# Dilated attention: 66 moving columns instead of 128 in the products of probabilities with v

## The reference, cut to what matters

```python
def _dilated_branch(q, k, v, window, dilation):
    ...
    sc = jnp.where(mask, sc, -jnp.inf)
    m = jnp.max(sc, -1)
    p = jnp.exp(sc - m[..., None])
    l = jnp.sum(p, -1)
    o = jnp.einsum('bhrnqk,bhrnkd->bhrnqd', p, vb.astype(F32)) / l[..., None]
```

## Time and profile before

| what | value |
|---|---|
| runs: median (lowest to highest of 3) | 2781.31 us (2777.66 to 2781.51) |
| profiled execution: span from first to last instruction | 2786.4 us |
| PE busy | 2702.5 us, 97% of the span |
| PEld busy | 2277.9 us, 82% |
| DVE busy | 2107.3 us, 76% |
| ACT busy | 1287.9 us, 46% |
| POOL busy | 343.9 us, 12% |

### The profile page before, as it was taken

The page is one execution under the profiler, slowest core; times in us unless marked ns, Lnnn a source line. Parts: engine busy times, 40 slices in busy tenths (PEclk is TensorE's granted clock), DMA queues, the critical chain, the costliest instruction groups (busy, mean ns, idle before and its releaser), DMA issues. The chain is left out here.

```text
span 2786.4 us, 44753 instructions
## 1 busy us (share of the span) xinstructions
PE 2702.5 (97%) x17355; PEld 2277.9 (82%) x17355; DVE 2107.3 (76%) x3262; ACT 1287.9 (46%) x2296; POOL 343.9 (12%) x273
## 2 busy tenths in 40 slices
PE   9999988989999999999999999899999999999998
PEld 7888877888888888888878887788877888888886
DVE  6644445775799999898889885366658999998978
ACT  5323345853454444443356754566543544444332
POOL 0000056340000000000000001365511000000001
PEclk9999999999999999999999999999999999999999
DMA  5323252534322222284322433532042122224652
GB/s 184 121 106 116 81 178 94 151 99 161 119 79 91 83 91 76 107 327 144 107 102 106 152 93 124 175 124 93 18 167 108 63 84 81 91 78 177 238 189 90
DMA packets 162444, 339.08 MB, mean 122 GB/s; under 512 B 35584, under 2 KB 69568, under 8 KB 151616
## 3 DMA queue, kind: packets, MB, share of 16 engines
q1 hardware_dynamic: 143664, 321.54, 32.6%
q10 hardware_dynamic: 18576, 14.75, 1.7%
HBM read 252.17 MB, written 84.05 MB: 121 GB/s over the span
## 5 line engine op out<-in xcount | busy, mean ns | idle before, releaser
L2494 POOL TENSOR_TENSOR ffn_down_rstd<-ffn_down_rstd,ffn_down_power 128x1 f32<-128x1 f32 x15 | 15.0, 1000 | 1263.2 <-DVE ffn_down_rstd L2430 1263.2
L1051 DVE TENSOR_TENSOR even_in_w_lo<-even_in_raw_left,even_in_w_hi 128x512 fp32r<-128x512 f32 x80 | 49.9, 686 | 88.2 <-ACT even_in_w_hi L976 88.2
L934 PE MATMUL even_in_acc<-even_in_w_hi,even_x_hi 128*128 128x512 f32 x256 | 99.6, 389 | 0.0
L935 PE MATMUL even_in_acc<-even_in_w_lo,even_x_hi 128*128 128x512 f32 x256 | 99.6, 389 | 0.0
L936 PE MATMUL even_in_acc<-even_in_w_hi,even_x_lo 128*128 128x512 f32 x256 | 99.6, 389 | 0.0
L4024 DVE SCALAR_TENSOR_TENSOR even_mixed<-even_mixed,odd_qkv_taps 128x1023 f32<-128x1023 f32 (+2 forms) x72 | 92.1, 1281 | 4.9 <-ACT even_mixed L3857 3.2
L3508 DVE CUSTOM_DVE_ANT_0 dil_probs<-dil_bank,dil_mask 128x128 f32<-128x128 f32 (+1 forms) x192 | 56.0, 347 | 38.9 <-PE dil_bank L3417 32.2
L936 PE MATMUL even_in_acc<-even_in_w_hi,even_in_s_lo 128*128 128x512 f32 x192 | 74.7, 389 | 0.0
L934 PE MATMUL even_in_acc<-even_in_w_hi,even_in_s_hi 128*128 128x512 f32 x192 | 74.7, 389 | 0.0
L935 PE MATMUL even_in_acc<-even_in_w_lo,even_in_s_hi 128*128 128x512 f32 x192 | 74.7, 389 | 0.0
L3464 ACT ACTIVATE dil_probs<-dil_probs,dil_neg_peak 128x128 f32<-128x128 f32 (+1 forms) x192 | 70.7, 442 | 2.6 <-DVE dil_neg_peak L3513 2.6
(11 more groups left out here) (881 smaller groups left out, 9221.1 us busy)
## 6 DMA issues: line engine op xcount, KB each, us to landing
ffn_w_raw<-in_ffn_up SPq DMA_DIRECT2D x42, 1024.0 KB, 4.8
even_mixed<-in_ffn_down SPq DMA_DIRECT2D x28, 512.0 KB, 4.1
odd_mixed<-in_ffn_down SPq DMA_DIRECT2D x28, 512.0 KB, 4.0
hp<-even_in_stage SPq DMA_DIRECT2D x13, 1024.0 KB, 4.2
hidden<-even_mixed SPq DMA_DIRECT2D x22, 512.0 KB, 2.6
ffn_w_raw<-in_od_w_qkv SPq DMA_DIRECT2D x11, 1024.0 KB, 5.7
hidden<-odd_mixed SPq DMA_DIRECT2D x22, 512.0 KB, 2.6
even_in_raw_left<-in_ev_w_in SPq DMA_DIRECT2D x10, 1024.0 KB, 5.0
```

Of the source, the lines that this page charges most:

```text
L934: pe.matmul(to, hi[:, tok], wh, start=(opens and k == 0), stop=False, skip_group_check=not opens)
L935: pe.matmul(to, hi[:, tok], wl, start=False, stop=False, skip_group_check=not opens)
L1051: dve.tensor_tensor(w_lo[:, p % 2, k], source(i)[:, k], f32(w_hi[:, p % 2, k]), ALU.subtract).then_inc(lo_ready, 1)
```

## The change

The window of v that streams past the stationary probabilities becomes 66 columns wide (`DIL_OUT`). An even head's window starts at its own first value (64 values, its ones, and the first value of the next head). An odd head's starts one column ahead of its first value, at the ones of the head before (those ones, 64 values, its own ones). The result goes to the first 66 columns of the head's place in PSUM, and the copy of the odd heads reads from column 1 instead of 63. The two lines with a matmul become a loop over the one or two blocks of keys, in the same order. The stationary operand, the number of matmuls, the semaphores and all other programs are as before.

```diff
         def v_window(u, h):
 
-            at = h // 2 * 2 * (DIL_HD + 1) + 2 * (h % 2)
-            return v[:, v_slot(u)].rearrange("p h e -> p (h e)")[:, at:at + P]
+            at = h // 2 * 2 * (DIL_HD + 1) + DIL_HD * (h % 2)
+            return v[:, v_slot(u)].rearrange("p h e -> p (h e)")[:, at:at + DIL_OUT]
...
-                    if has_before(u):
-                        pe.matmul(o_ps[:, h], probs_t[:, 2 * h], v_window(u - 1, h), start=True, stop=False)
-                    mm = pe.matmul(o_ps[:, h], probs_t[:, 2 * h + 1], v_window(u, h), start=not has_before(u), stop=True)
+                    for b in range(0 if has_before(u) else 1, 2):
+                        mm = pe.matmul(o_ps[:, h, 0:DIL_OUT], probs_t[:, 2 * h + b], v_window(u - 1 + b, h),
+                                       start=b == 0 or not has_before(u), stop=b == 1)
...
-                    at = parity * (DIL_HD - 1)
+                    at = parity
                     dve.tensor_copy(mine[:, :, 0:DIL_HD + 1], heads[:, :, at:at + DIL_HD + 1]).then_inc(o_copied, 1)
```

## The result

The changed kernel took 2789.55 us (median of 20 runs, 2775.21 to 2792.69), the kernel before 2781.69 us beside it (20 runs, 2775.95 to 2787.20). The ratio is 1.0022, with a 95% interval of 1.0014 to 1.0030: slower by 0.2%, where no change was forecast, and the median is 2.6 us above the range. The ratio is the one on record; the quotient of the two medians is 1.0028. A second measurement gave 1.0018 (1.0007 to 1.0030).

A forecast was written before the change was run, and what follows sets the result against it. PE was taken to bound the stage, with stationary loads setting its pace. All terms were taken as 0, leaving 2786.4 us on the profiled execution, 2781 us on the median's scale; range 2775 to 2787 us.

The forecast's parts named there:

- The pace: Products: the 128-column stationary load sets 112 ns a pass before and after, so 560 passes save 0 us.
- the rival of the moving stream: Products: the moving columns set the pace, 52 ns less a pass, 2752 to 2763 us; chance 0.06.
- The formula of the Trainium skill: Products: matmul gap (N / 2.4 + 2.5) ns, 56 for 128 columns and 30 for 66, giving about 2767 us.
- The group ends: Last product of each of 24 units: `o_done` 0.05 to 0.11 us earlier; taken as 0, bound -2.6 us.
- The clock step: Granted clock under the half filled stream: cost unknown, taken as 0; above, one or two more falls, 3.4 us.
- The clock rival: Eleven two-block units' product runs: clock falls in each, 11 x 1.7 = 19 us slower, 2800 us; chance 0.07.

The follow-up runs named there:

- the first profile: Profiled execution of the changed kernel (66 columns in all units) from its first measurement: 2786.1 us, ratio of that measurement 1.0022.
- the later three: Three more profiles of the unedited changed kernel, 66 columns in all units: 2792.56, 2789.61 and 2789.90 us.
- the filled gaps: Ten identity transposes in each of PE's two waits in units 22 and 23: ratio 1.0013 with 66 columns everywhere, 1.0009 in the kernel before.
- the two kernels next to it: Against the kernel before: 128 columns in the last three units and 66 in the other 21, 0.9990; 98 columns in all units, 0.9995.

## Why the prediction was wrong

**The pace** was right. Passes stay at 110 to 112 ns at full clock with 98, 66 and 34 moving columns and 128 stationary ones, so 560 x 0 ns was the sum; within a run the matmuls start 57 ns behind their loads, as foretold; and the rival of the moving stream (0.06) didn't come. The formula of the Trainium skill ("TensorE: Matmul & The Clock Gate", "Back-to-back issue gap") that was set beside it, which that section gives for single matmuls without their loads, is met by no run here: a pass with 34 columns takes as long as one with 128.

**The group ends** were right to within what a run can tell: unit 21 takes 7.65 us in both kernels, and nothing up to 597 us shows a wait that is new.

**The clock step failed.** It read "the cost is unknown: 0 below; above, one or two more falls at the places that are thin already (600 to 609 us), 3.4 us. I take 0." The place was named there, and the half filled stream as an unknown; the size and the choice were wrong. A fall was priced at 1.7 us, from a fall between 466 and 470 us after which a filled stream followed. Behind this one come units 22 and 23, whose stream is now half empty, and the lower clock stays: 7 x 0.49 / 0.5 + 7 x 0.48 / 0.5 = 13.6 us in the first profile and 20.4 us in the later three, at a cost of 5.6 us and of 7.6 us in the two units. The mean clock is low in 23 of 32 executions; that the fall at this place is behind all of them is a conclusion from the four that were profiled with it. With 128 or 98 columns a fall at the same place lasts 3.4 us and costs PE 1.7 us, the price that was put on it: unit 22's 32 passes take 5.4 us in place of 3.7, and unit 23 has its full clock. By DVE's copies it is 1.5 us (13.04 - 11.58). Part of each loss is hidden there: in the kernel before DVE came to these copies without a wait, so PE did not set the pace to the end of the stage, as the prediction had it.

**The clock rival** (0.07) was right that the clock decides and wrong where: not in the 11 long product runs, which keep 1.00 from 476 to 597 us, but at the end of the stage, where PE has no scores to fill its wait for ACT. Its argument against, that PE's loads and matmuls "follow each other without a gap", doesn't hold at that place, which the trace of before already showed as a wait. From 98 columns down the mean clock goes with them: 0.9933 at 98, 0.9908 at 66 (32 executions), 0.9863 at 34; the kernel before, with 128, has 0.9926. By the Trainium skill, Part 1 of the page "TensorE: Matmul & The Clock Gate", activity releases the clock; the traces agree in so far as falls with a filled stream behind them ended after 3.4 us, but no run here tells what counts as activity.

**What would have mended it**: to ask of the thin place not only whether a fall comes, but what stream stands behind it to end the fall.

**Left open**: why 66 columns up to unit 20 or 21 with 128 behind come out slightly faster than the kernel before (0.9990 and 0.9988, intervals just below 1); why 66 columns in the last two or three units alone cost less than 66 in all (1.0003 and 1.0011 against 1.0022); and where the filled gaps cost their time. The kernel with 128 columns in units 22 and 23 alone has the lowest ratio of all, but its interval overlaps those of the two kernels next to it (0.9990 and 0.9995).

## What to carry to other kernels

Fewer moving columns save nothing while the load of a full stationary operand sets the pace (here 110 to 112 ns for 128 float32 columns); look for the load's record before you shorten the stream. What the shorter stream takes away is PE's fill, which may be what keeps the clock up: check the places where PE waits between such runs, and keep the stream wide there. A loss of 0.2% that comes and goes between executions is found in the granted clock of each, and its place only in a profile of an execution that has it.

## What was not expected of the hardware

- PE can be busy by the profile (10.00 of 10 us) and yet keep the lower clock, 13.6 to 20.4 us in all, with 66 columns in a pass that has the time for 128. With 98 or 128 columns the clock came back within unit 22, after 3.4 us in each of three profiles.
- Executions of one kernel differ by 10 us (medians 2780.0 and 2790.3) according to their granted clock, 8.8 us of it from one place of 20 us.
- Twenty transposes put into PE's idle time came with 2.5 and 3.6 us more over the run (1.0009, interval from 1.0000, and 1.0013), at a mean clock no lower than before (0.9932 and 0.9937).
